# Who subtracts: the low halves of nine more weight blocks move from GpSimd to VectorE

## What is computed

```
h = rmsnorm(x, g_norm1) * (1 + sc1) + sh1           # adaLN; the context likewise
k, v, a, u, q, r, hy, gates = split(h @ w_in)       # 6688 columns
y_gla = gated linear attention, both directions, on k, v, q, decays from a, readout with r
y_s5  = S5 state space model, both directions, on u; then GELU and a GLU
y_hy  = Hyena: short convolution, then two long ones by a Fourier transform
mix   = sum_b sigmoid(gate_b) * (y_b @ w_br_b);     x += gate1 * (mix @ w_out)
x    += gate2 * SwiGLU(rmsnorm(x) ...);             out = rmsnorm(x, g_final)
```

## Time and profile before

| | before |
|---|---|
| median of three runs | 1237.23 us |
| profiled execution | 1236.0 us |
| its span | 1234.2 us |
| mean granted TensorE clock | 0.959 |

### The profile page before, as it was taken

How to read it: one execution, slowest core, us unless ns; L and a number is a source line. 1 busy time by engine, 2 the same in 40 slices (tenths; PEclk the granted TensorE clock), 3 DMA queues, 4 the chain that set the end, 5 groups by cost and what they waited for, 6 DMA issues and landing times.

```text
span 1234.2 us, 15806 instructions
## 1 busy us (share of the span) xinstructions
PE 1133.2 (92%) x6157; PEld 855.2 (69%) x6157; DVE 558.0 (45%) x1106; ACT 405.5 (33%) x766; POOL 329.3 (27%) x291
## 2 busy tenths in 40 slices
PE   4789989978989999998989999897999999999995
PEld 1358958866657776876535574696888888888884
DVE  3684156576488788784155646335000011000013
ACT  2572323543345544442511100234232212332221
POOL 3022312502200000000321010333555655655540
PEclk9889999988889999998999999898999999999998
DMA  9802223765133223232613036652333223333211
GB/s 326 281 27 76 69 69 126 128 153 170 37 92 95 78 78 94 78 95 80 202 47 124 14 113 231 208 166 71 96 83 94 94 94 102 103 102 102 69 53 68
DMA packets 139863, 135.36 MB, mean 110 GB/s; under 512 B 13178, under 2 KB 126106, under 8 KB 138765
## 3 DMA queue, kind: packets, MB, share of 16 engines
q1 hardware_dynamic: 126432, 105.51, 29.4%
q0 software_dynamic: 4256, 17.20, 3.8%
q10 hardware_dynamic: 9100, 11.64, 3.1%
HBM read 121.23 MB, written 11.01 MB: 107 GB/s over the span
## 4 chain that ended last, share of the span: by engine, by line
PE 58%; DVE 13%; issue 3%; ACT 2%; ACTq 1%; DVEq 0%; DMA 0%
PE psum L714 52%; PE psum L974 1%; DVE ring_lo L2023 1%; PE psum L747 1%; PE psum L967 1%; PE psum L954 1%; PE psum L942 1%; ACTq L1549 1%; PE psum L769 1%; DVE hT_lo L2333 1%; DVE buf L2168 1%; DVE buf L2099 1%; DVE buf L2150 0%; DVE buf L2069 0%; DVE buf L2072 0%
## 5 line engine op out<-in xcount | busy, mean ns | idle before, releaser
L1265 POOL TENSOR_TENSOR ring_lo<-buf,ring_hi 128x512 fp32r<-128x512 f32 (+2 forms) x212 | 269.0, 1301 | 466.9 <-ACT ring_hi L1420 466.9
L714 PE MATMUL psum<-hT_hi,ring_hi 128*128 128x512 f32 x712 | 284.8, 400 | 10.2 <-DVE hT_lo L2333 4.0
L714 PE MATMUL psum<-hT_lo,ring_hi 128*128 128x512 f32 x712 | 278.5, 391 | 0.0
L714 PE MATMUL psum<-hT_hi,ring_lo 128*128 128x512 f32 x712 | 278.5, 391 | 0.0
L1420 ACT ACTIVATE ring_hi<-buf 128x512 fp32r<-128x512 f32 (+1 forms) x260 | 139.7, 610 | 233.7 <-PE psum L714 161.1
L714 PE MATMUL psum<-buf,buf 128*128 128x512 f32 (+1 forms) x448 | 189.3, 580 | 13.6 <-DVE buf L2150 5.0
L714 PEld LDWEIGHTS psum<-hT_hi,ring_hi 128*128 128x128 f32 x712 | 134.5, 189 | 44.6 <-issue 9.1
L714 PEld LDWEIGHTS psum<-buf,buf 128*128 128x128 f32 x448 | 86.4, 195 | 106.7 <-issue 89.1
L714 PEld LDWEIGHTS psum<-hT_hi,ring_lo 128*128 128x128 f32 x712 | 134.4, 189 | 28.7
L714 PEld LDWEIGHTS psum<-hT_lo,ring_hi 128*128 128x128 f32 x712 | 134.6, 189 | 27.9 <-issue 1.4
L2342 DVE TENSOR_TENSOR buf<-psum,buf 128x512 f32<-128x512 f32 x22 | 15.2, 692 | 220.9 <-PE psum L714 220.9
(11 more groups left out here) (322 smaller groups left out, 1661.3 us busy)
## 6 DMA issues: line engine op xcount, KB each, us to landing
buf<-in_w_in SPq DMA_DIRECT2D x26, 1024.0 KB, 5.4
buf<-in_w_mod SPq DMA_DIRECT2D x24, 1024.0 KB, 7.0
buf<-in_w_ffn_in SPq DMA_DIRECT2D x44, 512.0 KB, 5.2
buf<-in_w_ffn_out SPq DMA_DIRECT2D x8, 1024.0 KB, 5.2
scr_k<-buf POOLq DMA_DIRECT2D x4, 1024.0 KB, 5.2
buf<-scr_k POOLq DMA_DIRECT2D x4, 1024.0 KB, 8.9
buf<-in_w_out SPq DMA_DIRECT2D x4, 1024.0 KB, 5.3
buf<-in_w_ffn_out SPq DMA_DIRECT2D x4, 768.0 KB, 4.5
```

The lines of the kernel that those rows point to most:

```text
L714: ins = nc.tensor.matmul(o, a, b, start=start and n == 0, stop=stop and n == len(pairs) - 1)
L1265: nc.gpsimd.tensor_tensor(ring_lo[:, a:a + n], ring[:, a:a + n], ring_hi[:, h + i * n:h + i * n + n].bitcast(fp32), SUB)\
```

## The change

```
         UNSPLIT = STEPS
-        loop_from, loop_to = STEPS.index(("s5_k", 0, 1)), STEPS.index(("s5_x", NB - 1, 1))
+        loop_from, loop_to = STEPS.index(("z",)), STEPS.index(("yinv", 1))
         on_vector, low_at = {}, {}
         for at, names in ahead.items():
             for name in names if loop_from < at < loop_to else []:
                 on_vector[name] = len(on_vector)
                 low_at.setdefault(min(at + 6, first_use[name]), []).append(name)
```

## The result

The changed kernel takes a median of 1285.18 us over four runs (1282.49 to 1286.8), the kernel before beside it 1237.6: 3.9% slower, ratio 1.0386 with a 95% interval of 1.0368 to 1.0404. The profiled execution took 1286.8 us, its span is 1284.3, 50.1 more than before. The forecast was 1280 in a range of 1264 to 1294.

What follows compares the result with a forecast made beforehand. PE, busy 92% of the span, plus its waits was taken as the bound. Net attention waits 30.2 us, Hyena 3.0 and clock 10 on 1236.0 gave 1279.2 profiled, forecast as a 1280 us median, range 1264 to 1294.

Steps and rivals of the forecast that it cites:

- r0: Block before rhalf 0: its subtraction stands behind gla_states 0 on DVE, so PE waits 7.4 us.
- r1: Block before rhalf 1: subtraction behind s5_angles and gla_cum 1, so PE begins 14.5 us later, 13.4 net.
- gate10: Block before merge_g 1 0 0: subtraction behind gla_out 3, a PE wait of 5.9 us, net 5.1 with 0.8 back.
- gate11 and hy0: Blocks ahead of s5_bc and merge_ev 1 2: covered by relief from POOL and DVE idle time, next to nothing and 0.
- u1: Block before chan u1: subtraction behind u_ev 1's copies on DVE, a new PE wait of 4.3 us.
- Hyena: gate21, gate22 and gate23: -1.0 us at the first filter step, +2.4 and +1.6 at the back transforms, together +3.0.
- The clock: PE at half clock behind the four new attention waits, 2.5 us each, +10 us; Hyena's two waits nothing in the sum.
- Rival C: Longer at half clock: four episodes at 3.7 us and Hyena's two waits at 2.5, giving 1289 us; chance 0.10.
- A: The clock holds in the new waits, giving 1269 us; chance 0.10.
- B: The later wait for the second direction's keys swallows 5.8 us of r1's cost, giving 1274 us; chance 0.07.
- D: Faster: relief from POOL in ufilt 0 0 0 (3.5 us) and gla_att 3 (0.8), 1232 us at best; chance 0.04.
- E: The window moves nothing, 212 subtractions still on POOL, or PE's wait isn't the new one; 1236 to 1237 us; chance 0.03.

Runs made afterwards that it cites:

- attn_only: The change limited to the six attention blocks u1, r0, r1, gate10, gate11 and hy0, Hyena's three staying on GpSimd; 1276.56 us, ratio 1.0327.
- clock_fill: The changed kernel, with PE doing 286 idle matmuls during its six waits, VectorE's lateness unchanged; 1270.01 us, ratio 1.026.
- early_all: All nine blocks on VectorE as in the change, but seven subtractions placed where VectorE idles before PE needs them; 1229.69 us, ratio 0.9941.
- hyena_only: The change limited to Hyena's three blocks gate21, gate22 and gate23, the attention part as in the kernel before; 1244.5 us, ratio 1.0051.
- after: The changed kernel itself, nine blocks' subtractions moved from GpSimd to VectorE; median 1285.18 us, ratio 1.0386 to the kernel before.
- only_gate22: The kernel before with gate22 alone moved to VectorE, into its idle time before yinv 0; 1232.01 us, ratio 0.9953.
- relief_two: The kernel before with gate10 (before gla_out 2) and gate22 (before yinv 0) moved to VectorE; 1230.76 us, ratio 0.9944.
- early_fill: early_all plus 44 and 40 idle PE matmuls before the 5.8 us keys wait and the 5.4 us wait ending S5's loop; 1226.12 us, ratio 0.9896.
- only_r1: The kernel before with r1 alone moved to VectorE, at the changed kernel's place behind gla_cum 1; 1252.32 us, ratio 1.0135.

## Why the prediction was right, and where its terms were off

**The reading of the queues** carried it. Of the four waits, three came out within 0.1 us: r0 7.4 forecast and 7.41 measured, r1 14.5 and 14.47, gate10 5.9 and 5.80, and the 0.8 that `gla_att 3` gives back was 0.85. gate11 and hy0 cost nothing that shows.

u1 was given 4.3 and took 3.3: I let the last copies of `u_ev 1` end 1.6 us after PE's last product, and they end 1.0 after. That is the chance stretch once more, which held PE up longer than DVE's chain; attn_only, with the same stretch of 10.2 us, has 3.3 as well. In clock_fill, whose stretch is as short as that of the kernel before, the copies end at 211.70, 1.6 us after PE's last product, and the subtraction at 214.19. PE's last product of `chan u0` and its first of `chan u1` there:

```profile
209.85 0.39 PE L725 MATMUL psum<-hT_hi,ring_lo 128*128 128x512 f32 x1
...
214.25 0.38 PE L725 MATMUL psum<-hc_hi,ring_hi 128*128 128x256 f32 x1 [1.14 <-DVE ring_lo L2035]
```

PE was done with `chan u0` at 210.07, where its idle matmuls begin, and had the block 4.2 us later. The term was right for the clock of the kernel before.

**A misreading of the earlier trace rows** did no harm: 5.8 us is the largest wait of PE in the attention stages, not in the kernel. The same list has 7.9 us for ACT (L778) and eight waits of 8.7 us together for DVE (L769); they are 7.9 and 8.9 after the change.

**Hyena** gave -1.1 at the first filter step (forecast -1.0), waits of 3.95 and 3.19 us before the back transforms (4.1 and 3.3), so +2.3 and +1.5 (2.4 and 1.6). As forecast, the filter operations of that step run at 0.68 us each.

**The clock** was the term that was mis-sized, in its places more than in its sum. For the four attention waits I put 10 us; the table has 1.3 + 2.3 + 1.4 + 2.1 = 7.1. For Hyena's two waits I put nothing, and they cost 2.5 + 1.4 = 3.9: behind the wait of 3.19 us PE ran at half clock, as it did behind the 3.32 us for u1. Together 11.0, beside which 10 looks well guessed and was so only by the errors cancelling. Rival C had those waits in it and too much elsewhere.

**Not in the sum** were 2.2 us at `wo 0` (the first product with w_out). PE waits 3.36 us there for POOL, where it waited for nothing before. In early_all and hyena_only, whose queues don't differ there, the wait is 3.4 and 3.3 us as well; the chain of waits of early_all names the load of the block ahead of ACT's and POOL's halves:

```profile
764.31 7.38 DMA buf<-in_w_out
...
772.49 4.94 POOL ring_lo L1267 x4
```

Ahead of it come modulation products on PE. In the kernel before they ran at half clock (775.0 to 785.3) and covered that chain; where they run at full clock PE is early and waits for it. The wait itself costs nothing: `wo 0` begins 11.2 us behind the first of those products before the change (774.59 to 785.75) and 11.1 after (822.43 to 833.52). What costs is the half clock behind it (832 to 839), which falls into the dense products of `wo 0`; this is read from the traces and wasn't tried. Nor is it clear that the change has part in it. The wait is there in after, hyena_only, early_all, only_gate22 (3.2 to 3.4 us) and relief_two (1.9), and missing or 0.2 us in the other seven of the twelve profiles, attn_only, clock_fill and early_fill among them, whose queues are the same there. It may be chance like the stretch at `chan u0`.

**The rivals.** A (the clock holds) fell with the windows above. B (the later wait swallows part of r1) fell with only_r1. D (relief makes it faster) named a true effect with the right price, 3.5 us at `ufilt 0 0 0`, and the wrong balance; its condition, DVE reaching the blocks before PE, is just what early_all meets, and there it holds: 7.6 us faster, where I had named 4.3. The half clock behind the 4.96 us wait, which I hadn't counted there, is gone with it (1.7 us); the rest of the difference lies within what the runs spread. E fell with the counts of L1265 and L2023.

**The tests that I had named** held, but for one that was too strict: that S5's loop and all behind Hyena stay unchanged. The loop is 1.4 us longer in the profile, inside the 3 us that I had allowed it, while one wait at its start grows from 3.86 to 4.20 us and is made up for before its end; one stretch at half clock in it is 6.8 us long and not 3.4, behind a wait of 2.8 us that both kernels have. The 2.2 us at `wo 0` are the other exception. The 40 us that I had named for the time ahead of the loop are there (40.2 behind the half clock of `merge_g 1 0 0`), but 4.7 of them are the chance stretches, so that agreement is partly luck.

## What to carry to other kernels

Work moved to an idle engine costs nothing for its own length and everything for its place: look up which step stands ahead of it in that engine's queue, when that step can end at the earliest, and when the consumer wants the result. A rule like "six steps later" that is nearly harmless inside a regular loop (before the change PE waited 1.6 us in all for its twelve blocks) can put 2.4 us of work behind 12 us of idle time elsewhere; give the planner the place of the input instead. To such a wait add what the clock takes from the products behind it, some 1.3 to 2.5 us for each of the six here, and if the wait can't go, matmuls that nobody reads can pay: about 10 us for the six waits here.

## What the runs showed of the hardware that I had not expected

Waits of PE of 3.2 to 14.5 us cost nearly the same behind them, 1.3 to 2.5 us, and most for one of the shorter ones (3.95 us, 2.5). With six waits filled by 286 idle matmuls the kernel was 15 us faster than with empty ones, of which about 10 can be placed at the waits. The half-clock stretch behind one and the same unchanged step is 3.4, 6.8 or 10.2 us in different executions, and behind a wait of 2.9 us in S5's loop it is 0, 3.4 or 6.8. The first is worth up to 3.4 us of a single profile (an estimate: half of 10.2 less 3.4), as much as separates some of these medians, so shifts between two profiles have to be read from behind such a place.
